# The r/k/v stage of a hybrid decoder step: two head pairs at a time, seven block products for each of k, r and v, half of the token shift on ScalarE, and two borders between later stages reordered

## The chip, the cores and the metric

The kernel runs on one core of one Trainium2 chip, in float32. The metric is the device time of one execution in microseconds (us), as the median of several runs. TensorE runs at one of two granted clocks, 1.2 or 2.4 GHz; the profile gives the granted clock of a stretch as a share of 2.4 GHz (PEclk).

## The reference, cut to what matters

One decoder layer: 512 prompt tokens and 8 sample tokens (T = 520 columns), model width 1024. The part that the change rebuilds makes the inputs of the RWKV-7 mixer from the normalised rows `xn`:

```python
proj = jnp.einsum('btd,dc->btc', xn, w_in)
prev = jnp.concatenate([shift0[:, None, :], cols[:, :-1]], axis=1)   # cols: the r, k, v and low-rank columns of proj
xs = cols + (prev - cols) * rwkv_mu
...
w_log = -jax.nn.softplus(-(w_bias + jnp.tanh(w_d) @ w_lora_up)) - 0.5
a = jax.nn.sigmoid(a_bias + a_d @ a_lora_up)
kk = (k * k_k).astype(f32).reshape(hs)
kk = kk / jnp.maximum(jnp.sqrt(jnp.sum(kk * kk, axis=-1, keepdims=True)), 1e-12)
k = k * (1.0 + (a - 1.0) * k_a)
y, wkv_new = wkv7_scan(wkv0, r_h, decay, k_h, v_h, -kk, kk * a_h)
bonus = jnp.sum(r_h * k_h * r_k, axis=-1, keepdims=True) * v_h
```

After it come the chunked scan, the gating branch A, the merge of both branches with two gates and their projections, and a mixture of 32 experts.

## The kernel before, in words

The program is a row of phases with a barrier of all engines between them: `phase_inputs` (norm, transposes, then the r/k/v stage), `phase_chunks` (the scan), `phase_gating`, `phase_merge`, `phase_tail`. Within a phase each engine runs its own list of instructions in order and waits on semaphores; nothing is reordered at run time.

The r/k/v stage holds tokens in the free dimension, as two halves of 260 columns, and channels in the partitions. The 1024 channels of each of r, k, v are 8 "head pairs" of 128. A loop takes two head pairs per turn. For one head pair TensorE runs `proj(0)` (r), `low_rank()` (two small products for decay and rate), `proj(1)` (k), `proj(2)` (v) and `head_sums()` (sums over each head of the squares of k and of r times k). A `project` is 16 matmuls of 128x128 weights on 260 columns; the profile shows each float32 matmul as two records, so 32. ScalarE copies each result out of PSUM (L502), does the two tanh (L507), a square (L516), a logarithm and an exponential for the norms (L521, L523: each needs its own table of functions, so a table load stands before each) and the two exponentials of the decay (L526, L528). VectorE does the token shift (`shift_mix`, L173, L174, L176), the scan of the decay (L625), the products `rkk` (L635), the norms (L643) and their use (L648, L651). GpSimd turns finished pairs into the first operands of the scan (`first_rows`, L187 to L190); the last four of these are on VectorE.

Gating and merge already use a scheme of seven products instead of eight. A "set" is two blocks of 128 output channels; weights and rows are cut in 2x2 blocks, `weight_sums` (GpSimd, L223 to L229) and four row sums `s1` to `s4` prepare sums of blocks, and TensorE runs seven `product`s of 4 matmuls (8 records) into three PSUM banks X, Y, W. In the order of TensorE: product 1 (X), 2 (Y), 3 (X), 4 (Y), 5 (W), 6 (Y), 7 (W). ScalarE copies bank X after product 1 (`t1`); VectorE's `u2`, `u3`, `c22`, `c21`, `c12` add banks and tiles after products 2, 4, 5, 6 and 7. Product 3 waits for `t1`, product 4 for `u2`, product 6 for `u3`, product 7 for `c22`, the next set's product 2 for `c21`, its product 5 for `c12`.

At the start of gating VectorE first makes the row sum `s3` (L1342), then sets a small constant (L1343) for which ScalarE waits before anything else. At the start of merge VectorE makes `first_sum` and `second_sum` of the rows of branch A (L1670, L1674) before `u2` of the first set (L1688), and `third_sum` and `fourth_sum` (L1678, L1682) behind it.

Of the kernel before, what the change touches and what calls it, by code (L numbers as in the profile page):

```python
# [9 lines left out]
ALU = mybir.AluOpType  # L10
# [3 lines left out]
P = 128  # L14
D = 1024
# [38 lines left out]
SETS = 3  # L54

# [22 lines left out]
RKV_STEPS = 2 * (3 * 3 + 2 + 2 + 1)  # L78
# [191 lines left out]

def phase_inputs(nc, m, a):

    ctx, sb, ps, sem = open_phase(nc)
    with ctx:
        w = sb("rk_w", [P, 2, 3, NK, P])
        lw = sb("rk_lw", [P, 2, P])
        cols = [sb(f"rk_cols{j}", [P, T + 1]) for j in range(3)]
        rate = sb("rk_rate", [P, T])
        tw = sb("rk_tw", [P, T])
        ta = sb("rk_ta", [P, T])  # L280
        kk2 = sb("rk_kk2", [P, T])
        rkk = sb("rk_rkk", [P, T])
        kx = sb("rk_kx", [P, T])
        norm = kk2
        carry = sb("rk_carry", [P, NC, CH + 1])
        ms = sb("x_ms", [P, NT + 1])
# [16 lines left out]
        s_w = [sem("r_w0"), sem("r_w1")]  # L303
        names = ("step", "proj", "cols", "zw", "za", "tw", "ta", "ss", "bo", "ss_read", "bo_read",
                 "kk", "kk2", "rkk", "r_used", "k_used", "v_used", "lw_used", "rate_used", "ln", "rn")
        (s_step, s_proj, s_cols, s_zw, s_za, s_tw, s_ta, s_ss, s_bo, s_ss_read, s_bo_read, s_kk, s_kk2,
         s_rkk, s_r_used, s_k_used, s_v_used, s_lw_used, s_rate_used, s_ln, s_rn) = \
            (sem("r_" + n) for n in names)
        used = [s_r_used, s_k_used, s_v_used]
        lo, hi = slice(0, HD), slice(HD, P)  # L310
        psx = [psp[0][:, 0], psp[0][:, 1], psp[1][:, 0], psp[1][:, 1]]
# [13 lines left out]
        s_ws, s_wm, s_wt, s_we = (sem("w_" + n) for n in ("ws", "wm", "t", "e"))  # L325

# [7 lines left out]
        def _(eng):  # L334
# [4 lines left out]
            eng.wait_ge(s_lt, 1)  # L339
            eng.tensor_scalar(m.gate_in[:, :], m.gate_in[:, :], 0.5, 0.5, ALU.mult, ALU.add).then_inc(s_lt, 1)  # L340
            eng.wait_ge(s_lt, 2)
            x = row_blocks(m.xT, m.xS)
# [2451 lines left out]
```

## Time and profile before

| what | value |
| --- | --- |
| median of 3 runs | 1149.79 us (1146.42 to 1149.85) |
| the profiled execution | 1150.46 us, its span 1148.70 us |
| TensorE busy in the span | 1043.4 us (91%) |
| VectorE, ScalarE, GpSimd busy | 543.5, 343.2, 357.5 us |
| r/k/v stage in the span | 35.3 to 231.1 us |
| scan, gating, merge start at | 231.1, 438.7, 569.2 us |

Times in rows are microseconds from the start of the span. The span is what the profiler saw of the engines; the execution takes 1.76 us more. "Busy" of TensorE is modelled from pipelined records: a record's duration overlaps the next, so the pace is read from starts.

### The profile page before, as it was taken

The numbers are of one execution on the slowest core, as the hardware profiler recorded it, in microseconds if no ns is written. First come the engines' busy times: TensorE is split into PE (matmuls) and PEld (weight loads), VectorE is DVE, ScalarE is ACT, GpSimd is POOL, SyncE is SP. The second block draws the span as 40 slices with busy tenths as digits, with TensorE's granted clock in tenths as the row PEclk, the third lists the DMA queues.
The fourth block names the chain that finished last, engine by engine and source line by source line (L and its number), as shares of the span: only waits on it lengthen the run. The fifth ranks groups of instructions, "written<-read, shape, count | busy, mean of one in ns | idle before, by whom it ended". The sixth has DMA issues, their size and how long they took to land. (4 is left out here: it accounts for less than half of the span.)

```text
span 1148.7 us, 25195 instructions
## 1 busy us (share of the span) xinstructions
PE 1043.4 (91%) x10525; PEld 794.1 (69%) x10525; DVE 543.5 (47%) x1235; ACT 343.2 (30%) x685; POOL 357.5 (31%) x409
## 2 busy tenths in 40 slices
PE   5999999789999898999999999999985999888783
PEld 5888888678888787888778888884553555454441
DVE  4555555645655643777654546434273322211126
ACT  3143333344555443444324461000111111111111
POOL 5201000144445522878553334520001222211110
PEclk9999999999999999999999999999996999988997
DMA  9033222030000007631124224315976999999965
GB/s 249 1 91 82 58 58 58 0 81 4 5 4 4 4 4 159 181 111 38 26 81 140 73 74 147 106 78 189 401 268 241 396 416 414 415 417 416 417 251 222
DMA packets 97414, 183.11 MB, mean 159 GB/s; under 512 B 10113, under 2 KB 72093, under 8 KB 88602
## 3 DMA queue, kind: packets, MB, share of 16 engines
q1 hardware_dynamic: 90653, 168.59, 41.3%
q0 software_dynamic: 5168, 8.56, 2.0%
q10 hardware_dynamic: 1485, 4.39, 1.0%
q8 instruction: 84, 1.38, 0.5%
q14 instruction: 24, 0.20, 0.1%
HBM read 173.24 MB, written 17.55 MB: 166 GB/s over the span
## 5 line engine op out<-in xcount | busy, mean ns | idle before, releaser
L197 PE MATMUL rk_ps<-xT,rk_w 128*128 128x260 f32 x768 | 172.6, 385 | 0.0
L197 PEld LDWEIGHTS rk_ps<-xT,rk_w 128*128 128x128 f32 x768 | 144.6, 190 | 26.9 <-issue 2.7
L2519 DVE SCALAR_TENSOR_TENSOR ex_sg<-tl_psA,ex_slot_rs,ex_sg 128x128 f32<-128x128 f32 x32 | 11.2, 351 | 141.2 <-ACT ex_sg L2319 141.0
L2011 POOL DMA_INDIRECT d_y<-tl_xn,ex_sidx x32 | 31.9, 996 | 121.3 <-DVE tl_xn L2523 107.6
L261 PE MATMUL psv<-xT,w_sum 128*128 128x260 f32 x256 | 64.0, 395 | 5.6 <-DVE g L1688 5.6
L2006 POOL DMA_INDIRECT tl_xn<-d_tok,ex_gidx x17 | 17.8, 1048 | 148.8 <-DVEq L2511 76.4
L261 PEld LDWEIGHTS psv<-xT,w_sum 128*128 128x128 f32 x256 | 49.7, 196 | 15.5 <-DVE g L1688 7.7
L187 POOL TENSOR_TENSOR ck_bk<-br_all,ck_pi 64x64 f32<-64x64 f32 x15 | 4.8, 319 | 166.2 <-DVE br_all L651 165.7
L804 PE MATMUL ck_b<-ck_X,ck_V 64*64 64x64 f32 x1280 | 52.2, 223 | 2.7 <-issue 2.0
L223 POOL TENSOR_TENSOR w_sum<-w 128x512 f32<-128x512 f32 x16 | 21.2, 1325 | 102.3 <-PE mg_w L261 102.0
L2319 ACT ACTIVATE ex_sg<-tl_psA,ex_slot_rs 128x128 f32<-128x128 f32 x32 | 11.8, 368 | 133.7 <-PE tl_psA L2177 133.7
L803 PE MATMUL ck_b<-ck_V,ck_X 64*64 64x64 f32 x1024 | 42.2, 222 | 6.7 <-issue 3.2
L804 PEld LDWEIGHTS ck_b<-ck_X,ck_V 64*64 64x64 f32 x1280 | 44.1, 134 | 5.2 <-issue 4.6
L992 DVE TENSOR_TENSOR ck_V<-psv,levels 128x256 f32<-128x256 f32 x40 | 17.0, 425 | 61.3 <-PE psv L790 60.9
L502 ACT ACTIVATE rk_cols<-rk_ps 128x520 f32<-128x520 f32 x24 | 14.6, 606 | 99.2 <-PE rk_ps L197 99.2
L803 PEld LDWEIGHTS ck_b<-ck_V,ck_X 64*64 64x64 f32 x1024 | 36.6, 134 | 10.2 <-issue 8.8
L2523 DVE COPY tl_xn<-psv 128x512 f32<-128x512 f32 x33 | 22.8, 692 | 34.5 <-PE psv L2187 34.5
L261 PE MATMUL psv<-xT,w_uv 128*128 128x260 f32 x128 | 31.9, 393 | 4.0 <-ACT uv_gv L1230 4.0
L928 ACT ACTIVATE ck_Z<-ck_b 128x256 f32<-128x256 f32 x64 | 24.5, 382 | 33.6 <-PE ck_b L803 32.6
L261 PE MATMUL psv<-xT,w 128*128 128x260 f32 x128 | 30.9, 384 | 0.0
L737 POOL TENSOR_TENSOR ck_bk<-br_all,ck_pi 64x512 f32<-64x512 f32 x14 | 17.7, 1267 | 42.0 <-ACT ck_pi L893 41.5
L261 PE MATMUL uv_psw<-xS,w_uv 128*128 128x260 f32 x128 | 30.7, 382 | 0.0
(583 smaller groups left out, 2533.5 us busy)
## 6 DMA issues: line engine op xcount, KB each, us to landing
wd<-in_moe_w_down SPq DMA_DIRECT2D x15, 1024.0 KB, 24.1
rk_w<-in_w_in SPq DMA_DIRECT2D x24, 512.0 KB, 6.1
tl_x<-in_moe_w_down SPq DMA_DIRECT2D x9, 1024.0 KB, 24.3
w_uv<-in_w_in SPq DMA_DIRECT2D x16, 512.0 KB, 5.4
w<-in_w_in SPq DMA_DIRECT2D x8, 1024.0 KB, 5.7
xT<-in_moe_w_gate SPq DMA_DIRECT2D x5, 1024.0 KB, 20.0
xT<-in_moe_w_up SPq DMA_DIRECT2D x5, 1024.0 KB, 24.0
bonus_all<-in_moe_w_gate SPq DMA_DIRECT2D x5, 1024.0 KB, 21.0
```

What stands on the lines that cost most here:

```text
L197: last = eng.matmul(out[:, h, 0:TH], weights[:, k, :], xT[:, k, h * TH:(h + 1) * TH], start=(k == 0), stop=(k == NK - 1))
L223: eng.tensor_tensor(w.t3, w.b22, w.b12, ALU.subtract).then_inc(sem, 1)
L261: ins = eng.matmul(bank[:, 0:TH], w[:, k, :], x[:, k, :], start=(first and k == 0), stop=(last and k == NK // 2 - 1), skip_group_check=True)
L502: eng.activation(split(cols[j][:, 1:T + 1]), halves(psp[(3 * h + j) % 2]), ACT.Copy).then_inc(s_cols, 1)
L737: eng.tensor_tensor(bk[rows, :, rows], m.br[rows, :, at], pi[rows, :, :], ALU.mult).then_inc(s_bk, 1)
L803: new_z = eng.matmul(b64(bank[g][2])[own, n, :], X[at, p, :], V[at, p, :], start=True, stop=True)
L804: new_x = eng.matmul(b64(bank[g][3])[other, n, :], V[at, p, :], X[at, p, :], start=True, stop=True)
L928: eng.activation(Z[:, grp(g), :], b64(bank[g][2]), ACT.Copy).then_inc(s_z_e[g], 1)
L992: eng.tensor_tensor(V[:, grp(g), :], b64(bank[g][1]), m.levels[:, lv + 1, :].unsqueeze(1).to_broadcast([P, GP, CH]), ALU.mult)\
L2006: eng.indirect_dma_start(out=xg[:, p % 2, :], out_offset=None, in_=m.d_tok, in_offset=bass.IndirectOffsetOnAxis(ap=gidx[:, p:p + 1], axis= ...
L2011: eng.indirect_dma_start(out=m.d_y2, out_offset=bass.IndirectOffsetOnAxis(ap=rows, axis=0), in_=yo[:, x, :], in_offset=None, bounds_check= ...
L2523: eng.tensor_copy(yo[:, out, :], psd[out]).then_inc(s_yo, 1)
```

## The change

Of the r/k/v stage nearly everything is written anew. The loops are unrolled: four turns of two head pairs, in each turn three sets in the order k, r, v (12 sets in all), each by the seven products of the later phases. The weights of a set (1 MB) are loaded in one transfer into one of three places. GpSimd makes the weight sums of set s + 1 while TensorE runs set s, and the row sums, `s3` among them, ahead of the stage. `low_rank` of the turn's two pairs stands behind products 4 and 5 of the k set, `head_sums` of the first pair behind product 3 and of the second behind product 4 of the v set. The token shift is halved: ScalarE multiplies the neighbour's column by mu (`shifted`, three small instructions), VectorE multiplies its own by 1 - mu and adds (`mixed`, one). Decay, rate and squares go from VectorE to ScalarE. The order on each engine is written out by hand. In gating the row sum `s3` is gone and ScalarE's wait for the constant moves into `root`. In merge the four sums of branch A's rows are spread behind `u2`, `u3`, `c22` and `c21` of the first set.

The diff, cut to its core:

```diff
+def rkv_blocks(m, w, s):
+
+    low, high = w[:, s % SETS, 0:NK // 2, :], w[:, s % SETS, NK // 2:NK, :]
+    half = NK // 2 * P
+    as_block = lambda flat, at: flat[:, at:at + half].rearrange("p (k c) -> p k c", c=P)
+    tail = (NP - 2) * T
+    if s == RKV_SETS - 1:
+        dead = w[:, (s - 2) % SETS, :, :].rearrange("p k c -> p (k c)")
+        sums = [as_block(dead, n * half) for n in range(3)]
+    elif s % 2 == 0:
+        sums = [as_block(m.v_flat, tail), as_block(m.v_flat, tail + half), as_block(m.wide[2], tail)]
+    else:
+        sums = [as_block(m.kk_flat, tail), as_block(m.kk_flat, tail + half), as_block(m.wide[1], tail + half)]
+    b12 = low[:, :, P:2 * P]
+    return Blocks(low[:, :, 0:P], b12, high[:, :, 0:P], high[:, :, P:2 * P], b12, *sums)
...
+            eng.wait_ge(s_w[0], 16)
+            weight_sums(eng, rkv_blocks(m, w, 0), s_wsum, 0)
+            eng.wait_ge(s_lp, 2)
             eng.tensor_tensor(x.s4, x.a12, x.s2, ALU.subtract).then_inc(s_row_sums, 1)
-            eng.wait_ge(s_row_sums, 3)
-            for pair in range(NP):
-                eng.wait_ge(s_ex, pair + 1)
-                eng.wait_ge(s_norm_used, pair + 2)
-                if pair < NP - 1:
-                    first_rows(eng, m, pair, lo, s_first)
-                first_rows(eng, m, pair, hi, s_first)
+            eng.tensor_tensor(x.s3, x.a11, x.a21, ALU.subtract).then_inc(s_row_sums, 1)
...
+            for s in range(1, RKV_SETS):
+                eng.wait_ge(s_w[s % SETS], 16 * (s // SETS) + 16)
+                if s > 1:
+                    eng.wait_ge(s_prod, 7 * (s - 1))
+                weight_sums(eng, rkv_blocks(m, w, s), s_wsum, 4 * s)
+                if s >= 4 and s % 3 == 1:
+                    eng.wait_ge(s_wsum, 4 * s + 4)
+                    for p in range(2 * (s // 3) - 2, 2 * (s // 3)):
+                        rows_of_pair(p)
+                    eng.wait_ge(s_first, 8 * 2 * (s // 3))
...
+            for s in range(SETS, RKV_SETS):
+                eng.wait_ge(s_prod, 7 * (s - SETS + 1))
+                load(s)
...
-                    eng.wait_ge(s_w[h], i * 80 + 80)
-                    proj(0)
-                    low_rank()
-                    proj(1)
-                    proj(2)
-                    head_sums()
...
+            def head_sums(p):
+                eng.wait_ge(s_kk2, p + 1)
+                eng.wait_ge(s_rkk, p + 1)
+                eng.wait_ge(s_za_read, p // 2 * 2 + 2)
+                if p % 2:
+                    eng.wait_ge(s_bo_read, p)
+                    eng.wait_ge(s_ss_read, p + 1)
...
+            for s in range(RKV_SETS):
+                b, p, sums, ws_done = rkv_blocks(m, w, s), s // 3 * 2, 5 * s, 4 * s
+                eng.wait_ge(s_w[s % SETS], 16 * (s // SETS) + 16)
+                if s:
+                    eng.wait_ge(s_xf, s)
+                product(eng, bank_x, b.b11, x.a11, last=False).then_inc(s_prod, 1)
+                eng.wait_ge(s_wsum, ws_done + 3)
+                if s:
+                    eng.wait_ge(s_sum, sums - 1)
+                else:
+                    eng.wait_ge(s_row_sums, 2)
+                product(eng, bank_y, b.t2, x.s2, last=False).then_inc(s_prod, 1)
+                eng.wait_ge(s_t1, s + 1)
+                product(eng, bank_x, b.b21, x.a12, first=False).then_inc(s_prod, 1)
+                if s % 3 == 2:
+                    head_sums(p)
+                eng.wait_ge(s_sum, sums + 1)
+                if s == 0:
+                    eng.wait_ge(s_row_sums, 4)
+                product(eng, bank_y, b.t3, x.s3, first=False, last=False).then_inc(s_prod, 1)
+                if s % 3 == 0:
+                    low_rank(p)
+                if s % 3 == 2:
+                    head_sums(p + 1)
+                if s:
+                    eng.wait_ge(s_sum, sums)
+                product(eng, bank_w, b.t1, x.s1, last=False).then_inc(s_prod, 1)
+                if s % 3 == 0:
+                    low_rank(p + 1)
+                eng.wait_ge(s_wsum, ws_done + 4)
+                eng.wait_ge(s_sum, sums + 2)
+                product(eng, bank_y, b.t4, x.a22, first=False).then_inc(s_prod, 1)
+                eng.wait_ge(s_sum, sums + 3)
+                product(eng, bank_w, b.b22, x.s4, first=False).then_inc(s_prod, 1)
...
+            def shifted(s, e):
+                c = at_row(s % 3, s // 3 * 2 + e)
+                mu, src = vec(m, "rwkv_mu")[:, c:c + 1], cols[s % 2][e]
+                eng.wait_ge(s_sum, 5 * s + 4 + e)
+                if e == 0:
+                    eng.wait_ge(s_xf, s + 1)
+                if s:
+                    eng.wait_ge(s_mixed, 2 * (s - 1) + e + 1)
+                eng.activation(m.shift_last[:, :, c], src[:, TP:T + 1], ACT.Copy)
+                eng.activation(before[e][:, TP:T], prev[:, c, :], ACT.Copy)
+                eng.activation(before[e][:, 1:TP], src[:, 1:TP], ACT.Copy, scale=mu).then_inc(s_before, 1)
...
+            for s in range(RKV_SETS):
+                p = s // 3 * 2
+                eng.wait_ge(s_prod, 7 * s + 1)
+                if s >= 2:
+                    eng.wait_ge(s_mixed, 2 * (s - 2) + 2)
+                eng.activation(cols[s % 2][0][:, late], bank_x[:, 0:TH], ACT.Copy).then_inc(s_t1, 1)
+                if s % 3 == 1:
+                    decays(p + 1)
+                    rate(p + 1)
+                    squares(p)
+                eng.wait_ge(s_prod, 7 * s + 3)
+                eng.activation(cols[s % 2][0][:, early], bank_x[:, 0:TH], ACT.Copy).then_inc(s_xf, 1)
+                if s % 3 == 0:
+                    tanh(p)
+                    decays(p)
+                    rate(p)
+                    shifted(s, 0)
+                    tanh(p + 1)
+                if s % 3 == 1:
+                    squares(p + 1)
+                    shifted(s, 0)
+                if s % 3 == 2:
+                    kept_sums(p)
+                    logs(p)
+                    roots(p)
+                    kept_sums(p + 1)
+                    logs(p + 1)
+                    shifted(s, 0)
+                    roots(p + 1)
+                shifted(s, 1)
+                if s % 3 == 2:
+                    for n in range(p, p + 2):
+                        exponentials(n)
...
+            def c12(s):
+                b = cols[s % 2][1]
+                eng.wait_ge(s_prod, 7 * s + 7)
+                eng.wait_ge(s_sum, 5 * s + 1)
+                eng.tensor_tensor(b[:, early], bank_w[:, 0:TH], b[:, early], ALU.add).then_inc(s_sum, 1)
+
+            def mixed(s, e, out):
+                c = at_row(s % 3, s // 3 * 2 + e)
+                eng.wait_ge(s_before, 2 * s + e + 1)
+                eng.scalar_tensor_tensor(out=out, in0=cols[s % 2][e][:, 1:T + 1], scalar=keep[:, c:c + 1], in1=before[e][:, :],
+                                         op0=ALU.mult, op1=ALU.add).then_inc(s_mixed, 1)
...
+            def products(p):
+                eng.wait_ge(s_mixed, 2 * (p // 2 * 3 + 1) + p % 2 + 1)
+                step.wait()
+                for own, other in ((lo, hi), (hi, lo)):
+                    last = eng.scalar_tensor_tensor(out=m.v[other, p, :], in0=m.r[own, p, :], scalar=vec(m, "r_k")[own, p:p + 1],
+                                                    in1=m.k[own, p, :], op0=ALU.mult, op1=ALU.mult)
+                last.then_inc(s_rkk, 1)
...
+            def norms(p):
+                eng.wait_ge(s_ss, p + 1)
+                eng.tensor_scalar(split(at_pair(m.bonus, p)), halves(pss), 1e-24, None, ALU.max).then_inc(s_ss_read, 1)
+
+            def scaled(p):
+                eng.wait_ge(s_rn, p + 1)
+                eng.scalar_tensor_tensor(out=at_pair(m.kk, p), in0=at_pair(m.kk, p), scalar=key[:, 0, p:p + 1],
+                                         in1=at_pair(m.bonus, p), op0=ALU.mult, op1=ALU.mult)
+                eng.scalar_tensor_tensor(out=at_pair(m.br, p), in0=at_pair(m.br, p), scalar=key[:, 1, p:p + 1],
+                                         in1=at_pair(m.bonus, p), op0=ALU.mult, op1=ALU.mult).then_inc(s_norm_used, 1)
...
+            for i in range(NP // 2):
+                p, s = 2 * i, 3 * i
+                if i:
+                    c12(s - 1)
+                    values(p - 2)
+                u2(s)
...
+                c12(s + 1)
+                received(p)
+                products(p)
+                u2(s + 2)
+                received(p + 1)
+                norms(p)
+                u3(s + 2)
+                products(p + 1)
+                c22(s + 2)
+                norms(p + 1)
+                scaled(p)
+                c21(s + 2)
+                scaled(p + 1)
...
                 if h == 0:
-                    eng.wait_ge(s_s3, 1)
                     eng.wait_ge(s_ws, 1)
...
             def root(h):
+                eng.wait_ge(s_eps, 1)
                 eng.wait_ge(s_mv, h + 1)
...
-            eng.wait_ge(s_eps, 1)
...
-            eng.tensor_tensor(x.s3, x.a11, x.a21, ALU.subtract).then_inc(s_s3, 1)
...
-                if p == 0:
-                    first_sum(a_rows)
-                    second_sum(a_rows, 0)
...
                 if p == 0:
-                    third_sum(a_rows, 0)
-                    fourth_sum(a_rows, 0)
+                    first_sum(a_rows)
                 if p == 1:
...
                 u3(i)
+                if p == 0:
+                    second_sum(a_rows, 0)
                 if p == NP:
...
                 c22(i)
+                if p == 0:
+                    third_sum(a_rows, 0)
...
                 c21(i)
+                if p == 0:
+                    fourth_sum(a_rows, 0)
```

## Rows read from the trace of the kernel before

**Rows 1.** Windows inside the stage: busy us of each engine (records), PEclk, DMA share, GB/s

```profile
143.60:172.30 28.70, 28.70 (x145) 23.75 (x144) 15.82 (x31) 9.03 (x14) 2.27 (x8) 1.00 0.22 58
```

**Rows 2.** Timeline of TensorE, one head pair: start us, length us, what

```profile
58.81 7.28 PE L197 MATMUL rk_ps<-xT,rk_w 128*128 128x260 f32 x32
...
67.10 14.29 PE L197 MATMUL rk_ps<-xT,rk_w 128*128 128x260 f32 x64
...
81.33 0.43 PE L456 MATMUL rk_pss<-rk_kk,ones 64*64 64x260 f32 x1
...
82.36 7.28 PE L197 MATMUL rk_ps<-xT,rk_w 128*128 128x260 f32 x32
```

**Rows 3.** Timeline of VectorE and ScalarE behind the same head sums

```profile
78.28 1.53 DVE L635 SCALAR_TENSOR_TENSOR rk_rkk<-r_all,vecs,k_all 64x520 f32 x2
...
82.48 0.70 DVE L643 TENSOR_SCALAR rk_kk<-rk_pss 128x520 f32<-128x520 f32 x1 [1.95 <-PE rk_pss L456]
...
83.35 0.64 ACT L521 ACTIVATE rk_kk<-rk_kk 128x520 f32<-128x520 f32 x1
...
84.00 1.28 ACT L523 ACT_TABLE_LOAD   x1
...
85.30 0.64 ACT L523 ACTIVATE rk_kk<-rk_kk 128x520 f32<-128x520 f32 x1
85.84 0.24 ACT L526 ACTIVATE ck_pi<-spare  x1
...
86.19 0.26 ACT L528 ACTIVATE spare<-spare  x1
```

**Rows 4.** Timeline across the end of the stage

```profile
223.35 0.38 PE L457 MATMUL rk_psz<-rk_rkk,ones 64*64 64x260 f32 x1
...
229.60 0.31 POOL L190 TENSOR_TENSOR ck_L<-r_all,spare 64x64 f32<-64x64 f32 x1
...
231.10 0.83 PE L845 MATMUL ck_b<-ident,shift_last 128*78 128x128 f32 x3 [7.37 <-PEq L120]
```

**Rows 5.** Timeline of the start of gating, and two products of its steady part

```profile
438.74 2.35 DVE L1342 TENSOR_TENSOR xT<-xT 128x1040 f32<-128x1040 f32 x1 [5.03 <-PEq L120]
...
441.15 0.39 ACT L1230 ACTIVATE uv_gv<-psv 128x260 f32<-128x260 f32 x1 [6.41 <-DVE uv_eps L1343]
...
441.59 2.55 PE L261 MATMUL psv<-xT,w_uv 128*128 128x260 f32 x8 [4.01 <-ACT uv_gv L1230]
...
459.70 1.92 PE L261 MATMUL uv_psw<-xS,w_uv 128*128 128x260 f32 x8
461.46 1.92 PE L261 MATMUL psv<-xT,w_sum 128*128 128x260 f32 x8
```

**Rows 6.** Windows behind two idle times of TensorE (gating, merge), columns as above

```profile
443.00:444.00 1.00, 1.00 (x4) 0.75 (x3) 0.00 (x0) 0.00 (x0) 0.92 (x2) 0.50 1.32 336
...
577.00:579.00 2.00, 2.00 (x5) 1.18 (x5) 2.00 (x2) 0.00 (x0) 1.92 (x2) 0.50 0.69 242
```

**Rows 7.** Timeline of the first set of merge

```profile
570.95 1.60 DVE L1670 TENSOR_TENSOR w_lo<-ya 128x1040 f32<-128x1040 f32 x1
571.02 1.92 PE L261 MATMUL psv<-xT,w 128*128 128x260 f32 x8
...
574.71 0.42 DVE L1688 TENSOR_TENSOR g<-psv,g 128x260 f32<-128x260 f32 x1
...
575.17 3.00 PE L261 MATMUL psv<-xT,w_sum 128*128 128x260 f32 x8 [2.24 <-DVE g L1688]
...
584.84 1.02 PE L1462 MATMUL mg_psn<-r_all,headones 128*128 128x512 f32 x2
```

**Rows 8.** One VectorE line of merge, forms with ns min/median/max

```profile
L1727 DVE TENSOR_TENSOR mg<-mg,g x4: 1761/1764/1769, 602.4 to 692.1; 128x520 f32<-128x520 f32 x4
...
L1727 DVE TENSOR_TENSOR g<-g x1: 695/695/695, 781.6 to 781.6; 128x520 f32<-128x520 f32 x1
```

**Rows 9.** Timeline around the weight sums of gating's third set

```profile
463.94 1.26 POOL L223 TENSOR_TENSOR w_sum<-w_uv 128x512 f32<-128x512 f32 x1 [16.47 <-DMA w_uv<-in_w_in]
...
468.51 1.92 PE L261 MATMUL psv<-xS,w_sum 128*128 128x260 f32 x8
```

More of the change, by code:

```diff
@@ L77 @@
 ROOT_STEPS = 2 * RSQRT_STEPS
-RKV_STEPS = 2 * (3 * 3 + 2 + 2 + 1)
 def rsqrt(eng, step, y, x, t):
@@ new lines, in head_sums @@
+            def head_sums(p):
[5 more added lines that the diff above has]
+                    eng.wait_ge(s_ss_read, p + 1)
+                for half in range(2):
+                    at = slice(half * TH, (half + 1) * TH)
+                    for own, other in ((lo, hi), (hi, lo)):
+                        ss = eng.matmul(pss[own, half, 0:TH], m.ones[own, 0:HD], m.bonus[own, p, at], start=True, stop=True)
+                        bo = eng.matmul(psz[own, half, 0:TH], m.ones[other, 0:HD], m.v[other, p, at], start=True, stop=True)
+                ss.then_inc(s_ss, 1)
+                bo.then_inc(s_bo, 1)
@@ new lines, in roots, with exponentials @@
+            def roots(p):
+                eng.wait_ge(s_ln, p + 1)
+                eng.activation(at_pair(m.bonus, p), at_pair(m.bonus, p), ACT.Exp, scale=-0.5).then_inc(s_rn, 1)
+            def exponentials(p):
+                eng.wait_ge(s_scan, p + 1)
+                eng.activation(m.pi[:, p, :], m.cum[:, p, 1:CH + 1], ACT.Exp, scale=-1.0).then_inc(s_pi, 1)
+                eng.wait_ge(s_pi, p + 1)
+                eng.activation(m.cum[:, p, 0:CH + 1], m.cum[:, p, 0:CH + 1], ACT.Exp).then_inc(s_ex, 1)
@@ L566, in _ @@
             step.did(eng.memset(xcols[:, :, 0:1], 0.0))
+            for n in range(2):
+                step.did(eng.memset(before[n][:, 0:1], 0.0))
+            step.did(eng.memset(decay[:, :], DECAY / 2))
             step.did(eng.tensor_scalar(m.half_bias[:, 0, :], vec(m, "w_bias"), 0.5, None, ALU.mult))
@@ new lines, in received @@
+            def received(p):
+                s = p // 2 * 3 + 1
+                mixed(s, p % 2, at_pair(m.r, p))
+            def products(p):
+                eng.wait_ge(s_mixed, 2 * (p // 2 * 3 + 1) + p % 2 + 1)
+                step.wait()
+                for own, other in ((lo, hi), (hi, lo)):
+                    last = eng.scalar_tensor_tensor(out=m.v[other, p, :], in0=m.r[own, p, :], scalar=vec(m, "r_k")[own, p:p + 1],
+                                                    in1=m.k[own, p, :], op0=ALU.mult, op1=ALU.mult)
+                last.then_inc(s_rkk, 1)
@@ L654, in _ @@
+            c12(RKV_SETS - 1)
+            for p in range(NP - 2, NP):
+                values(p)
             eng.wait_ge(s_ex, NP)
-            eng.wait_ge(s_norm_used, NP + 1)
+            eng.wait_ge(s_norm_used, NP)
             first_rows(eng, m, NP - 1, lo, s_first)
+            for p in range(NP - 2, NP):
+                bonus(p)
 def load_uv(eng, m, a, slot, h):
```

323 lines of the change are left out of this document (172 added, 151 removed).

## The prediction

> **What bounds the kernel now.** I read the page first: TensorE is busy 91% of the span, so a gain has to shorten TensorE's own line or take a wait off it. Next the windows of the r/k/v stage: TensorE is busy through all of a window at full clock, VectorE, ScalarE and GpSimd 55%, 31% and 8% of it [rows 1]. The stage is bound by TensorE. Its timeline gives the pace: head pairs start at 58.81 and 82.36, 23.55 us apart. Two projections take 67.10 to about 81.2, so 7.06 each; three are 21.18 and leave 2.37 for low rank and head sums. The head sums hold TensorE from 81.2 to the next product at 82.36, 1.15 [rows 2]. Then I read the waits of TensorE at the borders: 7.37 us at the end of the stage [rows 4], 4.01 at the start of gating [rows 5], 2.24 in the first set of merge [rows 7]. The seven-product scheme is to be seen in gating: a product starts 1.76 (1.755 over several) after the one before [rows 5].
>
> **The products.** A turn (two head pairs) had 6 projections, 42.36 us; it gets 21 products, 36.86. That is -5.5 a turn, -22.0 for four. Low rank and head sums keep their instructions. This gain stands only if nobody keeps TensorE waiting, so I lay the hand-written orders side by side. Terms: the end of a matmul reaches VectorE about 0.2 later (head sums end about 82.26, L643 starts 82.48), VectorE reaches ScalarE after 0.17 (83.18 to 83.35) [rows 3]; a bank add is 0.42 [rows 7], 0.35 to the start of the next.
>
> **A wait at the second head sums of every v set.** TensorE puts `head_sums(p + 1)` directly behind product 4. It needs `products(p + 1)`, which VectorE runs behind `u3`, and `u3` waits for product 4. So from the end of product 4 TensorE waits 0.2 + 0.35 + 1.53 (two L635) [rows 3] + about 0.15 for the hand-over = 2.25. Four times: +9.0. Behind the waiting head sums stand products 5 to 7, so nothing covers it.
>
> **A wait at the border from a v set to the next k set.** I follow the chain from the end of product 4 (time 0). Head sums end at 3.4, product 5 at 5.15. `c22` starts 5.35, `norms(p + 1)` (0.70) ends 6.4. ScalarE's logarithm (0.64) ends 7.2; its table load lies before. VectorE has `scaled(p)` ahead of `c21`: two of 0.70, then the add, 8.15. ScalarE's `shifted(s, 0)` waits for that add: two tiny copies and one of 512 columns; at 0.24 for a tiny one and 0.64 for a long one, overlapped as L521 to L528 are, 1.0, so 9.3. Only then comes the table load, 1.28, and the exponential `roots(p + 1)`, 0.64: 11.25 [rows 3]. `scaled(p + 1)` needs it, and in VectorE's order `c12` is behind: alone that is 12.65 for `scaled` and 13.0 for `c12`. But GpSimd is then at the weight sums of the next set. VectorE's L1727, both inputs in SBUF, takes 1.76 beside such sums and 0.70 without them [rows 8]. I put `scaled` at 13.75, `c12` at 14.1. `shifted(s, 1)` waits for `c12`: 15.3. Four exponentials of two pairs at 0.61 a pair: 16.5 [rows 3]. Then `t1`, 0.39 [rows 5]: 16.9. TensorE meanwhile has products 6, 7, 1, 2 and is done at 5.15 + 7.02 = 12.2; product 3 waits for `t1`. Wait 4.7 (3.6 without GpSimd's part, my lower end). Three borders: +14.1.
>
> Beside GpSimd's sums, `received` and `products(p)` in front of the first head sums end near 5.5 from the set's start where TensorE is there at 5.27: 0.25, three times, +0.8. The other sets I find covered: after the k set `t1` has about 0.8 us to spare, GpSimd makes a set's sums (four of 1.27 [rows 9]) a whole set (12.3) ahead, the load is issued two sets ahead. So the stage has no wait in k and r sets, and a turn takes 36.86 + 4.74 + 2.25 + 4.7 + 0.25 = 48.8 where before it took 47.1.
>
> **The table load against the skill.** The row shows the exponential starting 0.02 after the end of its 1.28 load, with nothing between [rows 3]. The Trainium skill (ScalarE: Activation LUTs, What ACT_TABLE_LOAD costs) gives 1.28 for the load and a further 1.38 for a drain at every switch, 2.66 in all; by it each of the three borders would wait about 1.4 longer, some 4 us in sum. The row decides for the sum; the other stands among the rivals.
>
> **The end of the stage.** Before, TensorE is done at about 223.7 and starts the scan at 231.10, 7.4 later; GpSimd's last row ends 229.91 and the barrier takes 1.2 [rows 4]. After, product 7 of the last set ends at 8.65 on the scale above. `scaled`, `c12` and `shifted(11, 1)` end at 14.1 here (no weight sums are left); the exponentials open GpSimd's twelve rows at 14.7, 0.3 each (L190) [rows 4]: 18.3; the barrier: 19.5. That is 10.85 behind product 7: +3.4. The bonus of the last pairs lies beside GpSimd.
>
> **The borders.** In gating ScalarE stood behind VectorE's 2.35 us sum and the constant; without it `t1` runs at 438.8 and product 3 at 439.2 instead of 441.59, -2.4, and the clock loss behind that idle time (below), -1.8: -4.2 [rows 5]. But the third set needs weights whose sums began only when the load had landed, at 463.94; the sum that product 2 needs is the third, done about 4.0 later, 467.9, and product 2 began at 468.51 [rows 9]. The load is issued earlier with the set, but behind 3.5 MB that the border issues at the same time as before. If it doesn't land earlier, 0.5 is left of the 4.2. I take -2.6, between. In merge `u2` waited behind two sums, 570.95 to 574.7; now product 4 follows product 3 at 572.8, and the sums fit behind `u3`, `c22`, `c21`. From 571.02 to 584.84 lie 9.64 us of work (5 products and a variance of 0.87), 2.39 of idle time, and 1.79 of slow clock [rows 7]: -4.2 at most. GpSimd's sums for the next set now run beside VectorE's and end up to 1.1 later, so -3.4.
>
> **The clock.** Behind the idle 4.01 and the idle 2.24 the granted clock stands at 0.50 (1.2 GHz) for a while [rows 6]; the merge case costs the 1.79 just found. The change makes seven new idle times of 2.25 to 4.7 in a stage that had none. At 0 to 1.79 each the sum is 0 to 12.5. I take 1.5 for the three long ones and 0.75 for the four that are as short as the shortest shown: +7.5.
>
> **Sum.** -22.0 + 9.0 + 14.1 + 0.8 + 3.4 + 7.5 - 2.6 - 3.4 = +6.8. On the profiled execution's own 1150.46 that is 1157.3. The median lies 0.67 below that execution, so 1156.6 on the median's scale. A change within 0.3% (3.4 us: 1146.3 to 1153.2) can't be told from none.
>
> **Rivals.**
> - *The waits come, the clock stays.* No row shows an idle time of this size inside dense products without a drop, but only two rows show one with it. Then 1156.6 - 7.5 = 1149.1, no change. Chance 0.22.
> - *ScalarE is in time at the border*, faster than before. Place: `t1` of the next k set. If `roots(p + 1)`, the copies and the exponentials were done before product 2 ends, 14.1 and its clock part of 4.5 go: 1138.0. It decides for faster once the border wait falls below about 1.3 each. For it: ScalarE's instructions of a turn add up to about 25 us of 48.8 by my count. Against it: the chain is of dependences, not of load, and each link has a row. Chance 0.14.
> - *The lock reaches further*: with GpSimd's sums beside the k and r sets, `u2` or `c22` is late there too. At 1.06 (1.76 - 0.70 [rows 8]) in each of eight sets, +8.5: 1165. Against it: those sets have 1.2 us or more in hand where I laid them out. Chance 0.09.
> - *A table switch holds ScalarE for twice its load* in the chain: another 1.28 at three borders, 3.8: 1160.4. The trace of before speaks against it (0.02 between). Chance 0.05. This is what the page above would do here.
>
> **How the numbers follow.** My own case has 0.50 and a range of 1151 to 1162 (border wait 3.6 to 5, clock 3 to 12, gating 0.5 to 4.2). To hold 8 in 10 the range takes in the case of the steady clock and leaves out the faster rival and the lock's: 1146 to 1163. Slower: six sevenths of my case, the last two rivals, a little of the first: 0.59. Same: the rest of mine, most of the first: 0.25. Faster: the second rival and the low end of the first: 0.16.
>
> **What would show it.** In the timeline after: a gap of about 2.2 us in front of every second `head_sums`, released by the VectorE products; a gap of 4 to 5 us in front of product 3 of sets 3, 6 and 9, released by ScalarE's copy of bank X, and behind it windows with PEclk 0.50; a stage from 35.3 to about 244; gating's first gap near 1.6 us, merge's gone. The forecast is wrong if the border gap is under 1.5 us, if no window of the stage shows the lower clock, or if gaps stand in k and r sets.

## The result

The changed kernel takes 1156.9 us in the median of six runs (1153.8 to 1162.9), the kernel before 1149.1. The ratio is 1.0078, with a 95% interval of 1.0053 to 1.0103: slower by 6 to 12 us. The forecast was 1156.6. The profiled execution took 1153.77 (span 1151.9); it is the fastest of the six, 3.1 below their median, and that matters below, where traces are added up.

The page of the profile after: TensorE's busy time went down by 14.3 us against the kernel before, and its share from 91 to 89%. The line PEclk (the granted clock in 40 slices of 28.8 us) has four slices at 8 or 7 among its first nine, which reach to 259 us and so hold the stage; in the kernel before all nine stand at 9.

```profile
PE 1029.1 (89%) x10429; PEld 781.4 (68%) x10429; DVE 563.4 (49%) x1195; ACT 375.7 (33%) x789; POOL 432.3 (38%) x458
...
PEclk9998988979999999999999999999996999989997
```

What TensorE waited for, from 30 to 620 us (total, times, longest). PEq is TensorE's own sequencer, here at the barrier between two phases; "issue" is idle time for which the profile shows no releaser:

```profile
PE rk_ps L262 <- ACT rk_cols L637: 15.4, 4, 4.0
PE ck_b L1063 <- PEq L121: 11.8, 1, 11.8
PE rk_pss L503 <- issue: 9.2, 7, 2.1
...
PE psv L262 <- ACT uv_gv L1446: 1.6, 1, 1.6
```

L637 is ScalarE's copy of bank X (`t1`). The prediction has three waits for it, and there are four. L503 is the first matmul of `head_sums`: four waits of 2.13 and three of 0.24. The profile names nobody for them; that it is VectorE's `products`, as the prediction has it, experiment 1 shows. The end of the stage is 11.8 instead of 7.4 [rows 4], gating's first wait 1.6 instead of 4.0 [rows 5], merge's wait [rows 7] is gone.

TensorE's timeline, the first of each kind (in square brackets the idle time ahead and what ended it):

```profile
42.78 2.02 PE L262 MATMUL rk_ps<-xT,rk_w 128*128 128x260 f32 x8 [3.33 <-ACT rk_cols L637]
...
77.32 0.40 PE L503 MATMUL rk_pss<-bonus_all,ones 64*64 64x260 f32 x1 [2.13 <-issue]
...
93.12 3.84 PE L262 MATMUL rk_ps<-xT,rk_w 128*128 128x260 f32 x8 [4.04 <-ACT rk_cols L637]
...
251.22 0.83 PE L1063 MATMUL ck_b<-ident,shift_last 128*78 128x128 f32 x3 [11.79 <-PEq L121]
```

The wait at 93.12 comes again at 144.64 and 196.00, so a turn takes 51.4 us. The windows around it (busy us of each engine, then the granted clock, DMA share, GB/s):

```profile
89.00:92.00 3.00, 0.08 (x1) 0.00 (x0) 3.00 (x3) 1.00 (x4) 2.67 (x2) 1.00 0.43 147
92.10:98.90 6.80, 5.78 (x13) 4.56 (x14) 2.04 (x4) 1.32 (x5) 5.35 (x16) 0.50 0.00 0
98.90:102.00 3.10, 3.10 (x18) 2.18 (x17) 1.03 (x2) 1.13 (x2) 0.00 (x0) 0.99 0.00 0
...
143.40:150.20 6.80, 5.56 (x13) 4.41 (x14) 2.27 (x4) 1.51 (x7) 5.34 (x16) 0.50 0.01 2
194.60:201.40 6.80, 5.40 (x13) 4.25 (x14) 2.42 (x4) 1.67 (x7) 5.38 (x17) 0.50 0.00 0
```

For 6.8 us the granted clock is 1.2 GHz. The first 1.0 us of that still lies in the wait; in the other 5.8 TensorE works, and half of that is lost: 2.9 us at the first border, 2.8 and 2.7 at the other two (5.56 and 5.40 us busy). The expectations of the experiments put it at half of 6.8, 3.4, which is too much. Border and clock together are 6.9 us a turn, where the products save 4.9 (worked out below).

Why `t1` is late at the border is read from ScalarE and VectorE:

```profile
82.45 0.69 DVE L807 TENSOR_SCALAR bonus_all<-rk_pss 128x520 f32<-128x520 f32 x1
...
84.39 0.42 DVE L762 TENSOR_TENSOR rk_cols<-rk_ps,rk_cols 128x260 f32<-128x260 f32 x1
...
87.75 1.17 DVE L811 SCALAR_TENSOR_TENSOR kk_all<-kk_all,rk_key,bonus_all 128x520 f32<-128x520 f32 x1 [2.94 <-ACT bonus_all L612]
88.85 1.78 DVE L813 SCALAR_TENSOR_TENSOR br_all<-br_all,rk_key,bonus_all 128x520 f32<-128x520 f32 x1
90.55 0.42 DVE L768 TENSOR_TENSOR rk_cols<-rk_ps,rk_cols 128x260 f32<-128x260 f32 x1
```

```profile
85.79 1.28 ACT L612 ACT_TABLE_LOAD   x1
87.08 0.64 ACT L612 ACTIVATE bonus_all<-bonus_all 128x520 f32<-128x520 f32 x1
91.00 0.22 ACT L628 ACTIVATE shift_last<-rk_cols 128x9 f32<-128x9 f32 x1 [3.28 <-DVE rk_cols L768]
...
92.53 0.26 ACT L618 ACTIVATE spare<-spare 128x65 f32<-128x65 f32 x1
92.70 0.37 ACT L637 ACTIVATE rk_cols<-rk_ps 128x260 f32<-128x260 f32 x1
```

It is the chain of the prediction link by link: norms, logarithm, `c21`, `shifted(s, 0)`, load, root, `scaled` beside GpSimd's additions (1.17 + 1.78 us, 0.75 each without), `c12`, `shifted(s, 1)`, four exponentials, `t1`. ScalarE itself stood idle for 3.28 us in the middle of it, with bank X ready since about 87.3, when product 1 had ended.

The wait that was not forecast is in the first set. VectorE and GpSimd there:

```profile
36.10 2.35 DVE L174 TENSOR_TENSOR br_all<-br_all 128x512 f32<-128x512 f32 x1 [1.93 <-ACT br_all L564]
38.38 2.34 DVE L175 TENSOR_TENSOR br_all<-shift_prev,br_all 128x8 f32<-128x8 f32 x1
40.75 0.76 DVE L177 SCALAR_TENSOR_TENSOR br_all<-br_all,vecs 128x520 f32<-128x520 f32 x1
```

```profile
35.51 2.40 POOL L370 TENSOR_TENSOR xS<-xT,xS 128x1040 f32<-128x1040 f32 x1 [3.47 <-PE rk_pss L467]
37.87 2.83 POOL L371 TENSOR_TENSOR xT<-xT 128x1040 f32<-128x1040 f32 x1
```

An addition over 8 columns takes 2.34 us: it ends at 40.72, with the second of GpSimd's row sums (40.70). ScalarE has the gate's tanh behind that shift, and `t1` behind the tanh. The trace of before had the same sign in another place: the shift's eight columns of r, beside a row sum of GpSimd from 43.92 to 46.65, where those of the low-rank rows, with GpSimd idle, took 0.16.

```profile
44.31 2.36 DVE L174 TENSOR_TENSOR r_all<-shift_prev,rk_cols 128x8 f32 x1
```

The Trainium skill (SBUF — State Buffer, SBUF: two separate sides) says that GpSimd and a VectorE instruction with two inputs in SBUF share a pair of ports, which one instruction holds for its whole length while the other blocks; the rows agree, even for eight columns.

### The profile page after: what moved, and what is told of

It reads as the page before. It is cut to its first block and busy times, and to the rows that moved or that the text cites. A ratio compares the mean times of both kernels' runs of the same rounds, so it can differ in the third digit from the quotient of the medians.

```text
span 1151.9 us, 24788 instructions
## 1 busy us (share of the span) xinstructions
PE 1029.1 (89%) x10429; PEld 781.4 (68%) x10429; DVE 563.4 (49%) x1195; ACT 375.7 (33%) x789; POOL 432.3 (38%) x458
## 3 DMA queue, kind: packets, MB, share of 16 engines
q8 instruction: 83, 1.36, 0.5%
## 5 line engine op out<-in xcount | busy, mean ns | idle before, releaser
L262 PE MATMUL rk_ps<-xT,rk_w 128*128 128x260 f32 x208 | 55.9, 416 | 15.4 <-ACT rk_cols L637 15.4
L262 PEld LDWEIGHTS rk_ps<-xT,rk_w 128*128 128x128 f32 x208 | 42.4, 207 | 24.3 <-ACT rk_cols L637 17.1
L2536 ACT ACTIVATE ex_sg<-tl_psA,ex_slot_rs 128x128 f32<-128x128 f32 x32 | 11.8, 367 | 131.0 <-PE tl_psA L2394 131.0
L262 PE MATMUL rk_ps<-xS,rk_w 128*128 128x260 f32 x200 | 50.4, 397 | 0.0
L262 PEld LDWEIGHTS rk_ps<-xS,rk_w 128*128 128x128 f32 x200 | 38.4, 195 | 8.6 <-issue 2.9
## 6 DMA issues: line engine op xcount, KB each, us to landing
xT<-in_moe_w_gate SPq DMA_DIRECT2D x5, 1024.0 KB, 20.1
```

Of the source, the lines that this page charges most:

```text
L262: ins = eng.matmul(bank[:, 0:TH], w[:, k, :], x[:, k, :], start=(first and k == 0), stop=(last and k == NK // 2 - 1), skip_group_check=True)
```

## The experiments

All edits but the eighth are to the changed kernel. Its median is 1156.9, with an interval of 1.0053 to 1.0103 of before; the scan's first matmul stands at 251.2 us in the first profile of it, and at 248.3 and 249.2 in two more (below).

**1. `products(p + 1)` early.**

```diff
-                norms(p)
-                u3(s + 2)
                 products(p + 1)
+                norms(p)
+                u3(s + 2)
```

> The changed kernel with one move on VectorE: in each v set products(p + 1), which the second head sums wait for, comes ahead of norms(p) and of u3. Theory (the step of 2.25 us a set in the prediction, 2.13 measured): the wait of TensorE before the second head sums goes in all four sets, 4 x 2.13 = 8.5 us, and with it the one stretch at 1.2 GHz that follows it (78.3 to 81.9 us, 1.8 us of loss); 1156.9 - 8.5 - 1.8 = 1146.6 us, and the border waits stay at 4.0 us. Rival: the chain of logarithm and root on ScalarE is what really bounds the set, and norms(p) now comes some 1.5 us later, so the border wait grows by what the head sums gain: 1156.9 us, border waits near 6 us.

1150.0 us (ratio to before 1.0016, 0.9996 to 1.0037), 6.9 less than the changed kernel. The waits before the head sums:

```profile
PE rk_ps L262 <- ACT rk_cols L637: 15.4, 4, 4.1
...
PE rk_pss L503 <- DVE bonus_all L807: 2.5, 3, 0.8
...
PE rk_pss L503 <- issue: 0.7, 3, 0.2
```

9.2 us of waits became 3.2; the border waits did not grow, so the rival is out. The theory missed that `norms(p)` frees the bank which the second head sums write: it is now later, and 0.8 of each wait stays in three sets. Of the 1.8 us for the clock the profile shows nothing gained: the slow stretch behind the first second head sums is gone, but one as long stands behind the first set's wait (42.2 to 45.6).

**2. The order on ScalarE.** `first_copy(s)` holds what stood at the head of the loop: the waits, the copy of bank X, and its `s_t1`.

```diff
+                if s % 3 or s == 0:
+                    first_copy(s)
...
                 if s % 3 == 2:
+                    exponentials(p)
                     kept_sums(p)
                     logs(p)
                     roots(p)
+                    exponentials(p + 1)
                     kept_sums(p + 1)
                     logs(p + 1)
+                    roots(p + 1)
                     shifted(s, 0)
-                    roots(p + 1)
+                    if s + 1 < RKV_SETS:
+                        first_copy(s + 1)
                 shifted(s, 1)
-                if s % 3 == 2:
-                    for n in range(p, p + 2):
-                        exponentials(n)
```

> The changed kernel with another order on ScalarE alone: roots(p + 1) ahead of shifted(s, 0), the copy of bank X of the next k set behind that and ahead of shifted(s, 1), and the exponentials of the two pairs early in the v set, where ScalarE idles. Theory: TensorE's wait at the border from a v set to the next k set (4.04 us, three times) is the queue of ScalarE; it goes, and the 6.8 us at 1.2 GHz behind each go with it (3.4 us of loss each): 3 x 7.4 = 22.3, and at the end of the stage the exponentials are no longer last, some 2 to 3 us: 1156.9 - 25 = 1132 us. Rival 1: the granted clock does not hang on the wait: 12 + 2.5 us go, 1142 us, and the stretches at 0.50 stay. Rival 2: product 4 of the k set then waits for u2 on VectorE, which is behind scaled(p + 1) and values(p) beside GpSimd's sums: the wait moves by one product and half of it stays, 1144 us.

1136.7 us (0.9903, 0.9885 to 0.9922): 20.2 less than the changed kernel, and faster than the kernel before. No instruction was taken away.

```profile
PE rk_pss L503 <- issue: 9.2, 7, 2.1
PE ck_b L1068 <- PEq L121: 7.2, 1, 7.2
PE rk_ps L262 <- ACT rk_cols L636: 3.3, 1, 3.3
PE rk_ps L262 <- DVE rk_cols L751: 1.6, 3, 0.5
```

Three border waits of 4.04 are now waits of 0.5 for `u2` (rival 2, but with 0.54 us left and not half of 4.04), the end of the stage is 7.2 instead of 11.8, and behind the borders the clock stays up. The scan starts at 228.8, 22.4 earlier, against the 25 expected: 10.5 of the border waits, 8.4 of the slow stretches behind them, 4.6 at the stage's end, and 0.9 as product 3 of the first set comes earlier, less 1.7 for a slow stretch that the first set's wait has in this execution.

**3. The fourth row sum early.**

```diff
+            eng.tensor_tensor(x.s4, x.a12, x.s2, ALU.subtract).then_inc(s_row_sums, 1)
             eng.wait_ge(s_lp, 2)
-            eng.tensor_tensor(x.s4, x.a12, x.s2, ALU.subtract).then_inc(s_row_sums, 1)
             eng.tensor_tensor(x.s3, x.a11, x.a21, ALU.subtract).then_inc(s_row_sums, 1)
```

> The changed kernel with GpSimd's fourth row sum (1040 elements, 2.4 us) ahead of its wait for the low-rank rows, so that only the third row sum is left beside VectorE's shift of the second low-rank column block. Theory: the 3.33 us that TensorE idles before product 3 of the first set come from the two sums, beside which VectorE's three instructions take 5.4 instead of 1.6 us; one sum less gives back 2.3 to 2.9 us: 1154.3 us, product 3 at about 40 us instead of 42.8. Rival: VectorE is late for another reason (its own order), or the early sum now slows the copy of the spatial weights by as much: 1156.9 us.

1154.3 us (1.0045, 1.0027 to 1.0063), 2.6 less. Product 3 of the first set in this kernel:

```profile
41.25 2.02 PE L262 MATMUL rk_ps<-xT,rk_w 128*128 128x260 f32 x8 [1.05 <-ACT rk_cols L637]
```

3.33 became 1.05: the first set's wait came from GpSimd's row sums. This is shown by the trace; the gain in time, 2.6, is not clear of the noise, as the two intervals overlap and the profiled execution is longer than the changed kernel's (1155.8 against 1153.8).

**4. A filler in the border wait.**

```diff
+                if s and s % 3 == 0:
+                    for n in range(2):
+                        product(eng, spare_bank, b.t2, x.s2)
                 eng.wait_ge(s_t1, s + 1)
```

> The changed kernel with two more products (16 matmuls, 3.5 us at full clock) on TensorE in each of the three border waits of 4.0 us, into a bank of PSUM that nothing reads. They take no time from the wait's end, which ScalarE sets. Theory: the 6.8 us at 1.2 GHz behind each border wait come from the engine's idling; with TensorE at work they go, 3 x 3.4 = 10 us: 1146.7 us, no stretch at 0.50 at the borders. Rival 1: the clock falls there for another reason: 1156.9 us, stretches stay. Rival 2: as theory, but the copy on ScalarE is late beyond the filler and the rest of the idle still brings the clock down in part: 1150 to 1155 us.

1151.7 us (1.0027, 1.0007 to 1.0048): 24 more matmuls, and 5.2 us less. (A product is 4 matmuls, 8 records: the two of a border are 8 matmuls and not 16, which are the records.) The border:

```profile
88.35 5.42 PE L262 MATMUL rk_ps<-xS,kk_all 128*128 128x260 f32 x24
94.30 2.02 PE L262 MATMUL rk_ps<-xT,rk_w 128*128 128x260 f32 x8 [0.53 <-ACT rk_cols L640]
```

```profile
92.00:99.00 7.00, 6.47 (x33) 4.84 (x31) 4.22 (x7) 2.39 (x9) 6.05 (x16) 1.00 0.00 0
```

The clock is at 2.4 GHz where it was at 1.2, at all three borders, so it was TensorE's idling that brought it down. From one border to the next it is now 48.6 us (94.30 to 142.94) instead of 51.5: 2.9 less, what the slow stretch had cost. In this execution the wait of the first set, which the filler leaves alone, had a slow stretch behind it with 6.0 us of work (3.0 lost) that the first profile of the changed kernel did not have; 8.4 - 3.0 = 5.4 is the distance between their scan starts (245.8 and 251.2). So a good half of the expected 10 us was had, and the slow stretch at the first set has the larger part of the rest.

**5. All moves.** The three above, and on VectorE `u2(s)` ahead of `values(p - 2)` and, at the stage's end, `first_rows` ahead of the last two `values`.

> The changed kernel with all three moves at once (products(p + 1) early; the order of ScalarE at the border; the fourth row sum early), and two more on VectorE: u2 of the k set ahead of values(p - 2), and the first rows of the last pair ahead of the last values. Theory: the three prices add, since each is a wait at another place: 6.9 + 20.2 + 2.6 us by the medians measured, 0.54 us for u2 at each of three borders, about 1.5 us at the stage's end: 1156.9 - 33 = 1124 us, the stage over at about 218 us instead of 251.2. Rival: with one wait gone the next one behind it shows (norms(p), now later, delays the logarithm and root; u3 and c22 come late in the v set), and a third of it is not had: 1134 us.

1124.1 us (0.978, 0.9749 to 0.9811), 2.2% faster than the kernel before (1.9 to 2.5). Up to the scan the trace accounts for it: the waits fell from 36.4 us to 11.1, and the 10.1 us of work lost to the slow clock are gone, 35.4 together, and the scan starts 35.5 earlier. Behind it this execution takes 7.2 us longer than the first profile of the changed kernel (scan 3.0, last stretch 4.2), and both scatter (9 to 12); so it is luck in part that the time came to the very 1124 of the sum. What is left of TensorE's waits in the stage:

```profile
PE ck_b L1068 <- PEq L121: 7.8, 1, 7.8
PE rk_pss L503 <- DVE bonus_all L812: 2.6, 3, 0.9
...
PE rk_psz L477 <- DVE wst L736: 1.0, 1, 1.0
PE rk_pss L503 <- issue: 0.7, 3, 0.2
```

The scan starts at 215.7. From one second head sums to the next it is 43.1 us (73.36, 116.44, 159.50), where a turn of the kernel before was 47.1. Waits of 0.24 and 0.85 are still in it; without them it is 42.0, and the new products are worth 5.1 a turn. The end of the stage gave nothing: 7.8, where experiment 2 had 7.2. There an operation of 64 columns took ten times its 0.3 us, beside VectorE's `values` and `bonus` (211.4 to 214.0):

```profile
210.81 0.32 POOL L189 TENSOR_TENSOR ck_bk<-k_all,ck_pi 64x64 f32<-64x64 f32 x1
211.08 3.14 POOL L190 TENSOR_TENSOR ck_L<-kk_all,spare 64x64 f32<-64x64 f32 x1
...
211.40 1.42 DVE L778 SCALAR_TENSOR_TENSOR v_all<-rk_cols,rk_keep,rk_before 128x520 f32<-128x520 f32 x2
212.74 1.29 DVE L830 TENSOR_TENSOR bonus_all<-rk_ta,v_all 128x520 f32<-128x520 f32 x2
```

**6. No table switch.** `ACT.Ln` in `logs` becomes `ACT.Square`. The kernel then leaves out the logarithm, so what it computes is another; it is of use for its time alone.

> The changed kernel with Square in place of the logarithm of the norms, so that the computation is another, with the same operands and shapes: if Square and the exponential share a table, the four table loads of a v set go. Theory: in the border chain only the load before roots(p + 1) stood (1.28 us), and the activation starts 0.02 us behind it; each border wait falls from 4.0 to 2.8 us and the stage's end from 11.8 to 10.5 us: 1156.9 - 4 x 1.3 = 1151.7 us, a little less where the shorter wait leaves the clock up. Rival (the Trainium skill, ScalarE: Activation LUTs, What ACT_TABLE_LOAD costs: a drain of 1.38 us beside the load's 1.28): 2.66 us at each of the four: 1146.3 us, border waits of 1.4 us.

1152.4 us (1.0034, 1.0014 to 1.0053), 4.5 less; the four loads of a v set are gone.

```profile
91.05 3.59 PE L262 MATMUL rk_ps<-xT,rk_w 128*128 128x260 f32 x8 [2.68 <-ACT rk_cols L637]
```

The border wait fell by 1.36 and the stage's end by 1.4 (11.8 to 10.4): one load of 1.28, and no further 1.38 for a drain. The time fell by less than the waits and the shorter slow stretches would give; its interval just touches the changed kernel's, so the reading rests on the waits. The rival, the drain of which the Trainium skill speaks (ScalarE: Activation LUTs, What ACT_TABLE_LOAD costs), is out.

**7. GpSimd's sums later.**

```diff
+                if s >= 4 and s % 3 == 1:
+                    eng.wait_ge(s_sum, 5 * (s - 1))
                 weight_sums(eng, rkv_blocks(m, w, s), s_wsum, 4 * s)
```

> The changed kernel with GpSimd's weight sums of the r set that follows a border held back until VectorE's c12 of the v set is done, some 4 us later; they are wanted only two sets on. Theory: what GpSimd's additions cost at the border is the stretch of scaled(p + 1), 1.17 + 1.78 us beside them and 0.75 + 0.75 without: 1.4 us of each border wait of 4.0 us, three times, 4.3 us: 1152.6 us, border waits of 2.6 us (the prediction put this part at 1.1). Rival: the held-back sums then lie beside values and bonus, u2 or u3 come late and product 4 or 6 waits instead: 1156.9 us or more.

1152.5 us (1.0029, 1.0009 to 1.0049), 4.4 less. The border waits are 2.60, 2.28 and 2.60, as the theory has it, and `scaled(p + 1)` takes 0.76 + 0.75. Behind these shorter waits the slow stretches are 3.4 us long instead of 6.8, which is not in the theory; but in this execution the first set's wait had one too, and in sum the slow clock costs the stage as much as before (9.8 us of work against 10.1).

```profile
92.95 3.68 PE L262 MATMUL rk_ps<-xT,rk_w 128*128 128x260 f32 x8 [2.60 <-ACT rk_cols L639]
```

**8. The borders alone, on the kernel before.** The four row sums of merge as in the change, and in gating:

```diff
             def root(h):
+                eng.wait_ge(s_eps, 1)
                 eng.wait_ge(s_mv, h + 1)
...
-            eng.wait_ge(s_eps, 1)
             for h in range(NP + 1):
```

> The kernel before with the border edits that can be had without the new stage: the merge stage's gate row sums one product later each, and in the gating stage the wait for eps moved from the first copy of bank X to the root; the third row sum itself stays on VectorE. Theory: the merge border gives 4.2 us (the whole second gap and its stretch at 1.2 GHz); in the gating stage product 3 starts at once and product 4 waits for the row sum, a gap of about 2.2 us instead of 4.0, and a shorter slow stretch behind it, 1.8 to 3 us: 1149.0 - 6.5 = 1142.5 us. Rival (the prediction's bound): what the merge order takes off the start it gives back where the row sums now lie: 0 to 1 us there: 1147 us.

1145.4 us (0.9968, 0.9943 to 0.9993), 3.4 less than before, half of what was expected; its interval reaches from 0.8 to 6.5. In the trace gating is 3.4 shorter than in three profiles of the kernel before (127.8 against 131.2) and merge 4.2 (211.7 against 215.9), and the last stretch 2.8 longer (370.5 against 367.7). The two borders together gave 7.6 us, more than the 6.5 expected; the last stretch, which the edit leaves alone, took 2.8 of it back in this execution.

```profile
438.94 2.02 PE L261 MATMUL psv<-xT,w_uv 128*128 128x260 f32 x8 [1.59 <-ACT uv_gv L1230]
441.53 1.99 PE L261 MATMUL psv<-xT,w_sum 128*128 128x260 f32 x8 [0.57 <-DVE uv_gu L1322]
```

So gating's gain comes from moving the wait for the constant; the row sum of 2.35 us, left where it was, costs 0.57.

**9 to 12. Each kernel twice more, unaltered.**

> The changed kernel once more, unaltered, for a second profile of it. In the first one the scan (from its first matmul to the gating stage's first product) takes 198.3 us against 202.8 in the kernel before, and the stretch from the last stage's first matmul to the end 363.8 against 368.2, though neither is changed. If these differ from execution to execution, a second profile shows other lengths (the scans of the kernels above lie between 198.3 and 202.8 us, the last stretches between 363.5 and 370.5), and the waits of the r/k/v stage are the same to 0.1 us. If the change shortens them, they are 198 and 364 us again.

> The kernel before once more, unaltered. Chance: a scan and a last stretch anywhere within 198 to 203 and 363 to 371 us. The change shortens them: 202 to 203 and 368 us or more, as in the first profile of it and in the kernel before with the border edits.

> The changed kernel a third time, as the second: chance gives lengths scattered over 198 to 203 and 363 to 371 us, an effect of the change gives 198 and 364 us each time.

> The kernel before a third time: chance gives scattered lengths, an effect of the change 202 to 203 and 368 us or more each time.

Starts of the sections in TensorE's timeline give these lengths in us (first profile, second, third). Gating and merge are counted here from TensorE's first product of each, 433.9 and 564.6 us in the kernel before, which it runs ahead of the barrier at 438.7 and 569.2:

```
                       before                  after                   difference of means
up to the scan         231.1  231.8  230.8     251.2  248.3  249.2     +18.3
scan                   202.8  203.5  201.8     198.3  199.0  202.0      -2.9
gating                 130.7  131.3  131.6     126.9  126.9  126.7      -4.4
merge                  215.9  215.9  215.9     211.7  211.7  211.7      -4.2
last stretch           368.2  367.2  367.8     363.8  364.3  364.0      -3.7
span                  1148.7 1149.7 1147.9    1151.9 1150.2 1153.7      +3.2
```

The waits of the r/k/v stage are the same to 0.1 us in all three profiles of the changed kernel (15.4, 11.8 and 9.2 in total). What differs up to the scan is the clock: the slow stretches cost 10.1, 7.1 and 9.4 us of work. The scan's code is unchanged, and its length scatters: 198.3 to 202.4 over the ten profiles of the changed kernel and its seven variants, 201.8 to 203.5 over four of the kernel before. The last stretch is 363.5 to 364.3 in eight of those ten, but 366.6 and 368.0 in experiments 7 and 5, and 367.2 to 370.5 in the four of before. Neither expectation holds cleanly: the scatter is there, and so is a shift of some 3 us in each.

## Why the prediction was right, and where it was not

The time was met within 0.3 us. Much of that is luck: up to the scan the change costs 20.1 us in the first profile and not the 12.8 of the terms, and the later sections give back 16.9 and not the 6.0 of the terms. The forecast of +6.8 lies between the +3.3 of that profile and the +7.8 of the medians.

- **The products**, -22.0. From the 20.1 take the waits (3.33, 8.5, 12.1, 0.7), the clock (10.1), the end (4.4) and the start (0.4): -19.4 is left, 4.9 a turn and not 5.5. I had priced all 21 products of a turn at the steady 1.755 from start to start. That holds between products (52.45 to 54.20), but a product that follows other work takes 1.86 (50.59 to 52.45, behind `low_rank`; 42.78 to 44.64, behind a wait).
- **Second head sums**, 2.25 each: 2.13, four times, 8.5 instead of 9.0. Experiment 1 takes most of it off.
- **The border**, 4.7 each: 4.04, 12.1 instead of 14.1. The chain was right (experiments 2, 6 and 7 each shorten it at the link they touch, by 3.5, 1.36 and, at its first border, 1.44 us).
- **First head sums**, 0.25: 0.24.
- **The stage's end**, 10.85: 11.79; +4.4 instead of +3.4. Experiment 2, which moves the exponentials and `roots(p + 1)` ahead, shows that ScalarE's order made it; it does not part the two.
- **The clock**, +7.5: 10.1 in the first profile (2.9, 2.8, 2.7 at the borders and 1.7 behind one of the four second head sums), 7.1 and 9.4 in the other two. With the products this is the term that was mis-sized most. I took 1.5 for the loss behind a border wait from a wait of 2.24 that loses 1.79 [rows 6, 7]; behind 4.04 it is 2.7 to 2.9. Its upper bound, 1.79 each, was too low there. That the clock depends on the wait at all, the first rival's question, experiment 4 settles.
- **The step that failed**: that the stage starts unchanged, and that "the stage has no wait in k and r sets". In the later sets that holds, but for the border waits, which the prediction priced by themselves. In the first set product 3 waits 3.33 us; a gap there is one of the prediction's own signs of being wrong. It comes because the change puts GpSimd's two row sums beside VectorE's last piece of low-rank work. I had used the slow rows [rows 8] at the border and not laid GpSimd's instructions beside VectorE's at the start. Experiment 3 shows the cause, and takes 2.28 us off the wait.
- **The borders**, -2.6 and -3.4: -4.4 and -4.2. Both came to the upper bound. In gating I feared that the third set would be bound by the landing of its weights [rows 9]; GpSimd's first sum of it now starts 26.4 us after gating's first product instead of 30.0, so the load moved with the set. In merge the row sums fit behind the products as laid out, and no clock drop is left.
- **Not in the sum**: scan and last stretch, -2.9 and -3.7 in the mean of three profiles. Their code is unchanged. Of the scan's 2.9, TensorE's idle time has 2.3 (15.8 to 13.5 in the mean); of the last stretch's 3.7, its idle time has 2.3 (59.3 to 57.0) and its busy time 1.5 (308.5 to 307.0), with the same matmuls, which fits the clock. Why there is less waiting and less slow clock stays open. In ten-microsecond windows of the last stretch the granted clock differs between kernels (0.89 in the window 310 us into it before, 1.00 after), with the loads at the same 392 and 394 GB/s there.
- The profiles put the change at +3.2 us in the mean and the timed runs at +7.8. I go by the timed runs, which are more; the three profiled executions of the changed kernel (1152.1, 1153.8, 1155.6) all lie below the median of its six runs. Why is open too.

Of the rivals, the steady clock is refuted by the windows at 0.50, and experiment 4 ties them to the idle time; ScalarE in time is refuted, but experiment 2 shows that it was one reordering away, and that the borders are worth 18.9 us in its trace (10.5 of waits, 8.4 of clock), close to the 18.6 that I gave it; the further reach of the lock was not seen where I had named it (no wait for `u2` or `c22` in k and r sets), but the lock did reach the first set; the longer table switch is refuted by experiment 6.

## What to carry to other kernels

When a stage of few long instructions is cut into many short ones, each engine's hand-written order has to be laid out again: the gain of some 20 us was there all along, and it was eaten above all by one queue in which a copy that frees the bound engine stood behind work that TensorE was not waiting for; putting that queue in order gave back 20.2 us. Price a wait of TensorE at its length plus the slow stretch behind it, which here cost another 1.7 to 3.1 us behind each wait of 4.0. And put the instructions of GpSimd and VectorE side by side wherever an edit moves either, at the first and last set too.

## What was unexpected of the hardware

- **Which idle times bring the clock down.** Over all 14 profiles, the idle times of TensorE between 40 and 600 us, and how many had windows at 1.2 GHz behind them: 0.8 to 1.6 us none of 83; 2.1 us 6 of 32; 2.2 to 2.3 us 4 of 4; 2.6 to 3.3 us 10 of 13; 4.0 us and more 32 of 32. Between 2 and 3.3 us the same wait in the same kernel does it in one execution and not in the next: the first set's 3.33 us in one of three profiles of the changed kernel.
- **The two engines block each other in both directions**, and a short instruction is held as long as a long one: 8 columns in 2.34 us on VectorE, 64 in 3.14 on GpSimd, which had to wait through four VectorE instructions in a row.
- **More work made the kernel faster**: 24 matmuls whose result nobody reads took 5.2 us off.
